# Row norms at stage ends: one matmul against a matrix of ones in place of two one-column matmuls, and the finished reciprocal root kept for all partitions

## The chip, the cores and the metric

One core of a Trainium2 chip runs the whole program. The metric is the device time of one launch in microseconds. The kernel before took 3085.26 us in the median of three runs (3084.18 to 3092.69). The two levels of the TensorE clock are 1.2 and 2.4 GHz; the profile gives them as 0.5 and 1.0 of the granted clock.

## The reference

Two network blocks follow each other on x of [256 tokens, 1024 features]. Each sublayer begins with an RMS norm over the features:

```python
def rmsnorm(x, g):
    xf = x.astype(jnp.float32)
    y = xf * lax.rsqrt(jnp.mean(xf * xf, axis=-1, keepdims=True) + RMS_EPS)
    return y.astype(x.dtype) * g

# first block, for two layers (mixers: hgrn + gmlp, then mla + moba attention)
x = x + mixer(x); x = x + peer_ffn(x, norm_ffn, ...)
# second block, for two layers (m are modulations; the layer-0 mixer reads a context ctx too)
x = x + 0.5 * m[2] * swiglu(modulate(x, norm_g[l, 0], m[0], m[1]), ffn1_wi[l], ffn1_wo[l])
x = x + m[5] * mixer(modulate(x, norm_g[l, 1], m[3], m[4]))      # window + gla, then a pooling mixer
x = x + 0.5 * m[8] * swiglu(modulate(x, norm_g[l, 2], m[6], m[7]), ffn2_wi[l], ffn2_wo[l])
return rmsnorm_2(x, final_g)
```

`modulate` is an RMS norm with a gain and a shift. The layer-0 swiglu ahead of the window mixer runs on the 256 rows of ctx as well.

## The kernel before

Features lie on partitions: x is `K.x`, [128, 8 chunks, 256 tokens] in SBUF, and stays there from start to end. The program is a sequence of stages. Each stage has its own semaphores and one instruction stream per engine, and all engines meet at a barrier between stages. Every big product is three fp32r products of high and low halves: ScalarE makes the high half of a weight tile with a copy (L262), VectorE or GpSimd the low half with a subtraction (L266), and TensorE multiplies (L2758, L2837 and others). Inside a stage TensorE is the engine that is always busy.

A norm needs, for each token, one over the root of the mean square over all 1024 features, and it needs that number on every partition, since tokens lie along the free axis. At nine places the sum of squares is made at the end of the stage that writes x (class `RowNorm`, slot 0 for x and slot 1 for ctx):

- VectorE writes a chunk of x (L3030, L2058, L797 or L3519); ScalarE squares it (L468); GpSimd adds chunks 0+1, 2+3 and 4+5 (L451).
- TensorE sums over the partitions (L461): for each of the three pairs and for chunks 6 and 7, two matmuls, one for each 128 tokens, with the squares as weights and one column of ones as the moving operand. The result is [128 tokens, 2]: a token lies on a partition.
- ScalarE takes the root of these 128x2 numbers (L472), VectorE the reciprocal (L476). Then comes the barrier.

In the next stage class `KnownNorm` spreads the result: TensorE multiplies a broadcast of the reciprocal with the identity (L418), which puts [128 partitions, 256 tokens] into PSUM. VectorE waits for that (L368) and then scales x chunk by chunk (L369): x times the gain times the spread reciprocal. ScalarE adds the shift and rounds to the high half (L357, or L262 where there is no shift), VectorE makes the low half of it (L382), in some stages GpSimd for the odd chunks (L266 and L393).

There are eight boundaries with such a norm: into `l_in`, `ffn1_0`, `wg_in` (two norms), `ffn2_0`, `ffn1_1`, `pool`, `ffn2_1` and `finish`. In the four `ffn` stages (function `swiglu`) ScalarE first makes the high halves of two weight tiles (L262, two of 128x1024) and then the chunks of the norm; GpSimd makes the low halves of these two weight tiles (L266, its only work there); TensorE multiplies the high parts chunk by chunk as the norm delivers them (function `highs`, L2758). Both `tensor` parts issue a few dummy products with the identity (`keep_awake`, L279), one at each stage's end and some at its start. In `l_in` and `wg_in` (function `project`) GpSimd makes the first weight tile's low half, and after it the odd chunks of the norm.

Of the kernel before, what the change touches and what calls it, by code (L numbers as in the profile page):

```python
# [17 lines left out]
P = 128  # L18
# [150 lines left out]
def setup(nc, keep, dram, K):  # L169

    taken = 0

    def sb(name, shape, dt=F32):
        nonlocal taken
        tile, size = padded(nc, keep, name, shape, dt, 64)
        taken += size
        return tile

    K.x = sb("x_stream", [P, DC, T])
    K.xp = sb("x_normed", [P, 2, DC, T], F32R)  # L180
    K.cols = sb("cols", [P, NCOL])
    K.ones = sb("ones", [P, P])
    K.ident = sb("ident", [P, P])
    K.iota = sb("iota", [P, P])
    K.eps = sb("eps", [P, 1])
    K.lb = sb("lower_bound", [P, AH])
    K.nlb = sb("one_less_lower_bound", [P, AH])
    K.mod = [sb(f"mod{n}", [P, MT, 2 - n]) for n in range(2)]
    K.row_root, K.row_inverse = sb("row_root", [P, 2, TT]), sb("row_inverse", [P, 2, TT])
    K.inv_freq = sb("inv_freq", [P, 32])  # L190
    K.cos, K.sin = sb("cos", [P, TT, 32]), sb("sin", [P, TT, 32])
    if (taken + MOVED) % LINE:
        sb("setup_end", [P, (LINE - (taken + MOVED) % LINE) // 4])

    K.raw = tile_in_lines(nc, keep, "raw", [P, RAWS, D])
    K.col = lambda name: K.cols[:, COL_AT[name][0]:COL_AT[name][1]]
    K.row = lambda name: K.rows[:, ROW_AT[name][0]:ROW_AT[name][1]]

    with stage(nc, K.stages, "setup") as st:
        cols_in, x_in, freq_in = st.sem("cols_in"), st.sem("x_in"), st.sem("freq_in")  # L200
        filled, v_step, exped = st.sem("filled"), st.sem("v_step"), st.sem("exped")
        cleared, shifted = st.sem("cleared"), st.sem("shifted")
        e = st.sb("e", [P, 3, AH])
        mx = st.sb("mx", [P, AH])
        mx2 = st.sb("mx2", [P, AH])
        spare = st.ps("spare", [P, P])
        block = st.ctx.enter_context(nc.Block())

        @block.tensor
        def _(pe):  # L210
            pe.wait_ge(filled, 1)
            keep_awake(pe, K, spare[:], 8)

        @block.sync
        def _(sp):
            sp.dma_start(K.cols[:], dram["cols"]).then_inc(cols_in, 16)
            sp.dma_start(K.x[:], dram["x"]).then_inc(x_in, 16)
            at = ROW_AT["inv_freq"]
            sp.dma_start(K.inv_freq[:], dram["rows"][at[0]:at[1]].partition_broadcast(P)).then_inc(freq_in, 16)
            sp.wait_ge(x_in, 16)  # L220
            sp.wait_ge(freq_in, 16)

        @block.gpsimd
        def _(pool):
            pool.memset(K.ones[:], 1.0)
            pool.memset(K.eps[:], EPS)
            pool.memset(K.ident[:], 0.0).then_inc(cleared, 1)
            pool.iota(K.iota[:], pattern=[[1, P]], base=0, channel_multiplier=0,
                      allow_small_or_imprecise_dtypes=True)
            pool.wait_ge(cleared, 1)  # L230
            pool.affine_select(out=K.ident[:], in_=K.ident[:], compare_op=ALU.not_equal, fill=1.0,
                               base=0, pattern=[[-1, P]], channel_multiplier=1).then_inc(filled, 1)

        @block.vector
        def _(dve):

            chain = Chain(dve, v_step)
            dve.wait_ge(cols_in, 16)
            lg = K.col("lb_logits").rearrange("p (r h) -> p r h", r=3)
            chain(dve.tensor_tensor(mx[:], lg[:, 0], lg[:, 1], ALU.max))  # L240
            chain(dve.tensor_tensor(mx2[:], mx[:], lg[:, 2], ALU.max))
            dve.tensor_tensor(e[:], lg, mx2[:].unsqueeze(1).to_broadcast([P, 3, AH]),
                              ALU.subtract).then_inc(shifted, 1)
            dve.wait_ge(exped, 1)
            chain(dve.tensor_tensor(mx[:], e[:, 0], e[:, 1], ALU.add))
            chain(dve.tensor_tensor(mx2[:], mx[:], e[:, 2], ALU.add))
            chain(dve.reciprocal(mx[:], mx2[:]))
            chain(dve.tensor_tensor(K.lb[:], e[:, 0], mx[:], ALU.mult))
            chain(dve.tensor_scalar(K.nlb[:], K.lb[:], -1.0, 1.0, ALU.mult, ALU.add))

        @block.scalar
        def _(act):
            act.wait_ge(shifted, 1)
            act.activation(e[:], e[:], ACT.Exp).then_inc(exped, 1)
# [27 lines left out]
class Norm:  # L282
# [67 lines left out]
    def scalar_to(self, act, end):  # L350
# [10 lines left out]
            ins.then_inc(self.cut, 1)  # L361
        self.scalar_at = max(self.scalar_at, end)

    def vector_scale(self, dve, end):

        for n in range(self.scaled_at, end):
            if n == 0:
                dve.wait_ge(self.spread, 1)  # L368
            dve.scalar_tensor_tensor(out=self.sq[:, n], in0=self.src[:, n], scalar=self.gain[:, n:n + 1],  # L369
                                     in1=self.rstd, op0=ALU.mult, op1=ALU.mult).then_inc(self.scaled, 1)  # L370
        self.scaled_at = max(self.scaled_at, end)
# [33 lines left out]
class KnownNorm(Norm):  # L405
# [2 lines left out]

    def __init__(self, st, K, tag, slot, *args, **kwargs):
        super().__init__(st, K, tag, *args, **kwargs)  # L410
        self.inverse = K.row_inverse[:, slot]

    def tensor_sums(self, pe, awake=3):
        pass

    def tensor_spread(self, pe):
        for t in range(self.tokens // P):
            mm = pe.matmul(self.rstd[:, t * P:(t + 1) * P], self.inverse[:, t:t + 1].to_broadcast([P, P]),  # L418
                           self.K.ident[:], start=True, stop=True, skip_group_check=True)
        mm.then_inc(self.spread, 1)  # L420

    def scalar_squares(self, act):
        pass
# [11 lines left out]
class RowNorm:  # L435
# [4 lines left out]

    def __init__(self, st, K, slot, src, sq, total):
        self.K, self.src, self.sq, self.total = K, src, sq, total
        self.root, self.inverse = K.row_root[:, slot], K.row_inverse[:, slot]
        self.stored, self.squared, self.paired, self.summed, self.rooted = (
            st.sem(f"rows{slot}_{x}") for x in ("stored", "squared", "paired", "summed", "rooted"))

# [6 lines left out]
    def tensor_sums(self, pe, c):  # L453
        if c < self.PAIRED:
            if c % 2:
                return
            pe.wait_ge(self.paired, c // 2 + 1)
        else:
            pe.wait_ge(self.squared, c + 1)
        for t in range(TT):  # L460
            mm = pe.matmul(self.total[:, t:t + 1], self.sq[:, c, t * P:(t + 1) * P], self.K.ones[:, 0:1],  # L461
                           start=c == 0 and t == 0, stop=c == DC - 1, skip_group_check=True)
        if c == DC - 1:
            mm.then_inc(self.summed, 1)

# [3 lines left out]

    def scalar_root(self, act):  # L470
        act.wait_ge(self.summed, 1)
        act.activation(self.root, self.total, ACT.Sqrt, bias=self.K.eps[:], scale=1.0 / D).then_inc(self.rooted, 1)  # L472

    def vector_root(self, dve):
        dve.wait_ge(self.rooted, 1)
        dve.reciprocal(self.inverse, self.root)  # L476


class LateNorm(Norm):
# [140 lines left out]
def project(nc, K, name, blocks, sources=lambda st: (), loads=(), ahead=None, ring=None, beside=None, rows=None, following=(),  # L620
# [11 lines left out]
    with stage(nc, K.stages, name) as st:  # L632
# [9 lines left out]
        src = sources(st)  # L642
        early = [s for s in src if not s.late]
        beside = beside and beside(st, src, evacuated, others)
        rows = rows and rows(st, acc[:, 0, 0:TT])
        following = Following(st, following)
        block = st.ctx.enter_context(nc.Block())

# [95 lines left out]
        def _(act):  # L744
# [32 lines left out]
            for b in range(b, len(blocks)):  # L777
                evacuate(b)
            if rows:
                act.activation(K.row_root[:, 0, 0:1], K.eps[:], ACT.Sqrt)  # L780
                for c in range(DC):
                    rows.scalar_square(act, c)
                rows.scalar_root(act)
# [461 lines left out]
def peer_experts(nc, K, name, layer, dram, raw, mix, beside, following):  # L1245
# [40 lines left out]
    with stage(nc, K.stages, f"{name}_e") as st:  # L1286
# [78 lines left out]
        iota_ps, w_low = out[:, 3, 0, 0:P], out[:, 3, 1]  # L1365
        norm_ps = out[:, 2].rearrange("p a t -> p (a t)")
        rstd, total = norm_ps[:, 0:T], norm_ps[:, T:T + TT]
        rows = RowNorm(st, K, 0, K.x, ring[:, 0:2].rearrange("p r (a t) -> p (r a) t", t=T), out[:, 0, 0, 0:TT])
        key_ps = g_ps[:, :, 0:TT * NK].rearrange("p k (t n) -> p k t n", t=TT)
        block = st.ctx.enter_context(nc.Block())  # L1370

# [1307 lines left out]
def swiglu(nc, K, name, wi, wo, streams, at, following=()):  # L2679
# [7 lines left out]
    with stage(nc, K.stages, name) as st:  # L2687
# [17 lines left out]
        def out_ps(s, c):  # L2705
# [5 lines left out]
                           total=acc[:, 7], all_vector=True)]  # L2711
        norms += [Norm(st, K, "n1", x.x, x.gain, x.shift, pair=x.pair, total=acc[:, 6], all_vector=True)
                  for x in streams[1:]]
        rows = [RowNorm(st, K, s, x.x, norms[s].sq, acc[:, 4 * s, 0:TT]) for s, x in enumerate(streams)]
        block = st.ctx.enter_context(nc.Block())

        @block.sync
# [744 lines left out]
def pool_mix(nc, K, dram, M, following):  # L3462
# [3 lines left out]
    with stage(nc, K.stages, "pool") as st:  # L3466
# [7 lines left out]
        acc = st.ps("acc", [P, DC, T])  # L3474
        h = a[:, :, pad:pad + T]
        norm = KnownNorm(st, K, "n", 0, K.x, M.gain(1), M.shift(1), raw=h)
        rows = RowNorm(st, K, 0, K.x, norm.sq, norm.total)
        following = Following(st, following)
        block = st.ctx.enter_context(nc.Block())

# [64 lines left out]
def second_block(nc, K, dram, mods, out):  # L3545
    for layer, M in enumerate(mods):
# [3 lines left out]
        if layer == 0:  # L3550
            with ExitStack() as keep:
                ctx = tile_in_lines(nc, keep, "ctx_stream", [P, DC, T])
                with ExitStack() as wide:
                    ctx_pair = moving_tile(nc, wide, "ctx_wide", [P, 2, DC, T])
                    swiglu(nc, K, "ffn1_0", *weights, [
# [114 lines left out]
```

## Time and profile before

| | |
|---|---|
| median of three runs | 3085.26 us |
| the profiled execution's own time | 3088.12 us |
| its span | 3086.4 us |
| TensorE busy | 3031.7 us, 98% |
| VectorE busy | 2095.9 us, 68% |
| ScalarE busy | 1582.3 us, 51% |
| GpSimd busy | 605.3 us, 20% |
| mean granted TensorE clock | 0.982 |

The span is that of the profiled execution, first to last instruction; the 1.7 us beside it lie around it. Busy times of TensorE are modelled ends of pipelined matmuls, so 98% busy does not say that it is at its peak in every stage. An fp32 matmul (L461, L418, L279, L3531) appears as two records, an fp32r matmul as one.

### The profile page before, as it was taken

How to read it: one execution, taken by the hardware profiler on the slowest of the kernel's cores; microseconds unless marked ns; L12 is line 12 of the kernel's file. 1: busy time of each engine (PE TensorE's matmuls, PEld its weight loads, DVE VectorE, ACT ScalarE, POOL GpSimd, SP SyncE). 2: the span in 40 equal slices, each digit the busy share in tenths (PEclk: the TensorE clock that was granted, in tenths of full speed). 3: DMA queues.
4: the chain of work that ended last, by engine and by line, in shares of the span. 5: the costliest groups of instructions: out<-in, count | busy, mean ns of one | idle time of the engine just before them, and what ended most of it. 6: DMA issues, size and time to landing. Idle time of an engine off the chain costs nothing. (4 is left out here: it accounts for less than half of the span.)

```text
span 3086.4 us, 66249 instructions
## 1 busy us (share of the span) xinstructions
PE 3031.7 (98%) x25756; PEld 2962.7 (96%) x25756; DVE 2095.9 (68%) x3612; ACT 1582.3 (51%) x2760; POOL 605.3 (20%) x327
## 2 busy tenths in 40 slices
PE   9899999999999999999999999999999899999998
PEld 9799999999999799999999999999998799999898
DVE  4669788789996659888778886333255555555654
ACT  5364577655555654577655554222145354454443
POOL 1126377600001016477500000000020000000100
PEclk9999999999999999999999999999999899999999
DMA  5256655688896256655689994223242246565464
GB/s 189 81 162 186 183 164 163 197 260 288 288 370 204 88 158 194 191 164 162 191 286 317 312 318 148 90 95 93 91 117 76 73 148 194 171 192 176 144 196 144
DMA packets 172777, 560.62 MB, mean 182 GB/s; under 512 B 22480, under 2 KB 31440, under 8 KB 172000
## 3 DMA queue, kind: packets, MB, share of 16 engines
q1 hardware_dynamic: 172640, 558.83, 56.3%
q8 instruction: 82, 1.34, 0.2%
q14 instruction: 55, 0.45, 0.0%
HBM read 557.71 MB, written 1.05 MB: 181 GB/s over the span
## 5 line engine op out<-in xcount | busy, mean ns | idle before, releaser
L262 ACT ACTIVATE peer_e_hi<-raw 128x1024 fp32r<-128x1024 f32 x560 | 590.5, 1055 | 313.6 <-PE peer_e_out L1558 256.3
L266 DVE TENSOR_TENSOR ffn_lo<-raw,ffn_hi 128x1024 fp32r<-128x1024 f32 x256 | 312.9, 1225 | 470.8 <-ACT ffn_hi L262 470.8
L262 ACT ACTIVATE ffn_hi<-raw 128x1024 fp32r<-128x1024 f32 x264 | 279.2, 1061 | 531.5 <-PE ffn_acc L2843 337.4
L266 POOL TENSOR_TENSOR peer_e_lo<-raw,peer_e_hi 128x1024 fp32r<-128x1024 f32 x198 | 478.0, 2416 | 286.2 <-ACT peer_e_hi L262 285.6
L266 DVE TENSOR_TENSOR peer_e_lo<-raw,peer_e_hi 128x1024 fp32r<-128x1024 f32 x362 | 444.3, 1227 | 119.6 <-ACT peer_e_hi L262 115.8
L1554 PE MATMUL peer_e_out<-x_normed,peer_e_hi 128*128 128x256 f32 x2048 | 493.6, 283 | 0.0
L1555 PE MATMUL peer_e_out<-x_normed,peer_e_hi 128*128 128x256 f32 x2048 | 481.7, 278 | 0.0
L1624 PE MATMUL peer_e_out<-peer_h_pair,peer_e_hi 128*128 128x256 f32 x2048 | 477.7, 276 | 0.4 <-DVE peer_e_lo L266 0.4
L1625 PE MATMUL peer_e_out<-peer_h_pair,peer_e_hi 128*128 128x256 f32 x2048 | 477.5, 276 | 0.0
L1555 PEld LDWEIGHTS peer_e_out<-x_normed,peer_e_hi 128*128 128x128 f32 x2048 | 385.8, 188 | 0.0
L1554 PEld LDWEIGHTS peer_e_out<-x_normed,peer_e_hi 128*128 128x128 f32 x2048 | 385.3, 188 | 0.2 <-issue 0.2
L1624 PEld LDWEIGHTS peer_e_out<-peer_h_pair,peer_e_hi 128*128 128x128 f32 x2048 | 384.4, 188 | 0.7 <-issue 0.7
L1625 PEld LDWEIGHTS peer_e_out<-peer_h_pair,peer_e_hi 128*128 128x128 f32 x2048 | 384.5, 188 | 0.0
L2838 PE MATMUL ffn_acc<-x_normed,ffn_hi 128*128 128x256 f32 x1280 | 313.5, 277 | 0.0
L2837 PE MATMUL ffn_acc<-x_normed,ffn_hi 128*128 128x256 f32 x1280 | 313.4, 277 | 0.0
L262 ACT ACTIVATE peer_h_pair<-peer_e_h 128x256 fp32r (+1 forms) x256 | 106.8, 418 | 334.6 <-PE peer_e_out L1628 334.6
L1558 PE MATMUL peer_e_out<-x_normed,peer_e_lo 128*128 128x256 f32 x2048 | 276.6, 277 | 0.5 <-POOL peer_e_lo L266 0.5
L1628 PE MATMUL peer_e_out<-peer_h_pair,peer_e_lo 128*128 128x256 f32 x2048 | 276.0, 276 | 0.0
L1558 PEld LDWEIGHTS peer_e_out<-x_normed,peer_e_lo 128*128 128x128 f32 x2048 | 253.2, 188 | 1.3 <-POOL peer_e_lo L266 0.9
L1628 PEld LDWEIGHTS peer_e_out<-peer_h_pair,peer_e_lo 128*128 128x128 f32 x2048 | 252.1, 188 | 0.0
L2837 PEld LDWEIGHTS ffn_acc<-x_normed,ffn_hi 128*128 128x128 f32 x1280 | 240.8, 188 | 0.0
L2838 PEld LDWEIGHTS ffn_acc<-x_normed,ffn_hi 128*128 128x128 f32 x1280 | 240.6, 188 | 0.0
(640 smaller groups left out, 6136.7 us busy)
## 6 DMA issues: line engine op xcount, KB each, us to landing
raw<-in_l_down SPq DMA_DIRECT2D x256, 512.0 KB, 3.6
raw<-in_l_up SPq DMA_DIRECT2D x256, 512.0 KB, 4.8
raw<-in_ffn_wi SPq DMA_DIRECT2D x176, 512.0 KB, 3.7
peer_e_ring<-in_w_mod SPq DMA_DIRECT2D x144, 512.0 KB, 5.3
raw<-in_ffn_wo SPq DMA_DIRECT2D x88, 512.0 KB, 3.6
raw<-in_l_peer_w_query SPq DMA_DIRECT2D x32, 512.0 KB, 3.5
raw<-in_w_in SPq DMA_DIRECT2D x26, 512.0 KB, 4.2
l_in_raw<-in_l_w_in SPq DMA_DIRECT2D x24, 512.0 KB, 4.4
```

The lines of the kernel that those rows point to most:

```text
L262: return act.activation(hi, v, ACT.Copy)
L266: return eng.tensor_tensor(lo, v, hi.bitcast(F32), ALU.subtract)
L1554: pe.matmul(out, w, K.xp[:, 0, c], start=c == 0, stop=False)
L1555: pe.matmul(out, w, K.xp[:, 1, c], start=False, stop=False)
L1558: mm = pe.matmul(out, lo[:, k % 2, c * P:(c + 1) * P], K.xp[:, 0, c], start=False, stop=c == DC - 1)
L1624: pe.matmul(out[:, c, 0], w, h_hi[:, k % 2], start=first, stop=False, skip_group_check=True)
L1625: pe.matmul(out[:, c, 0], w, h_lo[:, k % 2], start=False, stop=False, skip_group_check=True)
L1628: return pe.matmul(out[:, c, 0], lo[:, k % 2, c * P:(c + 1) * P], h_hi[:, k % 2], start=False, stop=False, skip_group_check=True)
L2837: pe.matmul(at, w, x.pair[:, 0, c], start=c == 0 and s == 0, stop=False, skip_group_check=True)
L2838: pe.matmul(at, w, x.pair[:, 1, c], start=False, stop=False, skip_group_check=True)
```

## The change

The matmuls of `RowNorm.tensor_sums` are turned round: the whole 128x128 matrix of ones is the weight and the squares stream through it, 256 columns, so every partition receives the sum of every token. Root and reciprocal are then taken of 128x256 numbers. The result is kept in SBUF (`K.row_rstd`, 1 KB a partition for x; another for ctx), and `KnownNorm` uses it as it lies: its spread matmuls and VectorE's wait for them are gone, and L369 reads the reciprocal root from SBUF instead of PSUM. Places that only follow (PSUM rooms of 256 columns instead of 2) are left out below.

```diff
-    K.row_root, K.row_inverse = sb("row_root", [P, 2, TT]), sb("row_inverse", [P, 2, TT])
+    K.row_rstd = [sb("row_rstd", [P, T])]
...
+    def wait_rstd(self, dve):
+        dve.wait_ge(self.spread, 1)
+
     def vector_scale(self, dve, end):
         for n in range(self.scaled_at, end):
             if n == 0:
-                dve.wait_ge(self.spread, 1)
+                self.wait_rstd(dve)
             dve.scalar_tensor_tensor(out=self.sq[:, n], in0=self.src[:, n], scalar=self.gain[:, n:n + 1],
                                      in1=self.rstd, op0=ALU.mult, op1=ALU.mult).then_inc(self.scaled, 1)
...
 class KnownNorm(Norm):
-        self.inverse = K.row_inverse[:, slot]
+        self.room, self.rstd = self.rstd, K.row_rstd[slot][:]
     def tensor_spread(self, pe):
-        for t in range(self.tokens // P):
-            mm = pe.matmul(self.rstd[:, t * P:(t + 1) * P], self.inverse[:, t:t + 1].to_broadcast([P, P]),
-                           self.K.ident[:], start=True, stop=True, skip_group_check=True)
-        mm.then_inc(self.spread, 1)
+        pass
+    def wait_rstd(self, dve):
+        pass
...
 class RowNorm:
-        self.root, self.inverse = K.row_root[:, slot], K.row_inverse[:, slot]
+        self.rstd = K.row_rstd[slot][:]
     def tensor_sums(self, pe, c):
-        for t in range(TT):
-            mm = pe.matmul(self.total[:, t:t + 1], self.sq[:, c, t * P:(t + 1) * P], self.K.ones[:, 0:1],
-                           start=c == 0 and t == 0, stop=c == DC - 1, skip_group_check=True)
+        mm = pe.matmul(self.total, self.K.ones[:], self.sq[:, c], start=c == 0, stop=c == DC - 1,
+                       skip_group_check=True)
     def scalar_root(self, act):
-        act.activation(self.root, self.total, ACT.Sqrt, bias=self.K.eps[:], scale=1.0 / D).then_inc(self.rooted, 1)
+        act.activation(self.rstd, self.total, ACT.Sqrt, bias=self.K.eps[:], scale=1.0 / D).then_inc(self.rooted, 1)
     def vector_root(self, dve):
-        dve.reciprocal(self.inverse, self.root)
+        dve.reciprocal(self.rstd, self.rstd)
```

## Rows read from the trace of the kernel before

**Rows 1.** The page, busy time, share and instructions of TensorE and VectorE.
```profile
PE 3031.7 (98%) x25756; PEld 2962.7 (96%) x25756; DVE 2095.9 (68%) x3612; ACT 1582.3 (51%) x2760; POOL 605.3 (20%) x327
```

**Rows 2.** Line view of L476: durations in ns, then what VectorE waited for (us, times).
```profile
L476 DVE RECIPROCAL row_inverse<-row_root x9: 166/166/168, 957.8 to 3076.2; 128x2 f32<-128x2 f32 x9
...
  ACT row_root L472: 21.6, 9
```

**Rows 3.** Timeline of TensorE, ffn2_0 into ffn1_1: start, us, line, [idle before <-releaser].
```profile
2671.48 2.15 PE L461 MATMUL ffn_acc<-ones,ffn_n_sq 128*128 128x1 f32 x12 [0.18 <-POOL ffn_n_sq L451]
...
2674.56 1.20 PE L418 MATMUL ffn_acc<-ident,row_inverse 128*128 128x128 f32 x4 [0.30 <-PEq L146]
...
2676.99 3.30 PE L2758 MATMUL ffn_acc<-x_normed,ffn_hi 128*128 128x256 f32 x16 [0.38 <-ACT x_normed L357]
```

**Rows 4.** Timeline of ScalarE, the same boundary.
```profile
2673.67 0.26 ACT L472 ACTIVATE row_root<-ffn_acc,eps 128x2 f32<-128x2 f32 x1 [2.25 <-PE ffn_acc L461]
2674.54 2.00 ACT L262 ACTIVATE ffn_hi<-raw 128x1024 fp32r<-128x1024 f32 x2 [0.61 <-PEq L146]
2676.45 3.29 ACT L357 ACTIVATE x_normed<-ffn_n_sq,mod 128x256 fp32r<-128x256 f32 x8
```

**Rows 5.** Timelines of VectorE and GpSimd, the same boundary.
```profile
2673.96 0.17 DVE L476 RECIPROCAL row_inverse<-row_root 128x2 f32<-128x2 f32 x1 [3.00 <-ACT row_root L472]
2675.80 3.22 DVE L369 SCALAR_TENSOR_TENSOR ffn_n_sq<-x_stream,mod,ffn_acc 128x256 f32<-128x256 f32 x8 [1.67 <-PE ffn_acc L418]
2678.93 4.52 DVE L382 SCALAR_TENSOR_TENSOR x_normed<-ffn_n_sq,mod,x_normed 128x256 fp32r<-128x256 f32 x8
...
2675.67 4.72 POOL L266 TENSOR_TENSOR ffn_lo<-raw,ffn_hi 128x1024 fp32r<-128x1024 f32 x2 [4.24 <-ACT ffn_hi L262]
```

**Rows 6.** Line views of VectorE's reciprocals L518 and L1968: ns min/median/max, shapes.
```profile
L518 DVE RECIPROCAL hgrn_heads_rstd<-hgrn_heads_root x1: 203/203/203, 128.8 to 128.8; 128x8 f32<-128x8 f32 x1
...
L1968 DVE RECIPROCAL peer_e_dens<-peer_e_dens x2: 253/253/253, 363.5 to 1287.4; 128x16 f32<-128x16 f32 x2
```

**Rows 7.** Timeline of TensorE: last sums at the pool boundary; fp32 matmuls of 256 columns.
```profile
2859.81 1.50 PE L461 MATMUL ffn_acc<-ones,ffn_n_sq 128*128 128x1 f32 x12 [0.18 <-POOL ffn_n_sq L451]
...
2877.69 1.99 PE L3531 MATMUL pool_acc<-pool_pooled,pool_w 128*128 128x256 f32 x8 [1.17 <-DVE pool_pooled L3514]
```

**Rows 8.** Line view of L3531: ns min/median/max of one record.
```profile
L3531 PE MATMUL pool_acc<-pool_pooled,pool_w x32: 379/379/483, 2874.6 to 2884.0; 128*128 128x256 f32 x32
```

**Rows 9.** Line views of L369, L382 and GpSimd's L266, start of ffn2_0.
```profile
L369 DVE SCALAR_TENSOR_TENSOR ffn_n_sq<-x_stream,mod,ffn_acc x8: 472/473/480, 2487.5 to 2490.2; 128x256 f32<-128x256 f32 x8
...
L382 DVE SCALAR_TENSOR_TENSOR x_normed<-ffn_n_sq,mod,x_normed x8: 472/472/1739, 2490.6 to 2494.7; 128x256 fp32r<-128x256 f32 x8
...
L266 POOL TENSOR_TENSOR ffn_lo<-raw,ffn_hi x2: 2374/2383/2392, 2487.4 to 2489.7; 128x1024 fp32r<-128x1024 f32 x2
```

**Rows 10.** Timelines of VectorE and GpSimd at the start of peer1.
```profile
1066.12 2.74 DVE L266 TENSOR_TENSOR x_normed<-peer_mix,x_normed 128x256 fp32r<-128x256 f32 x3
...
1065.00 4.46 POOL L266 TENSOR_TENSOR x_normed<-peer_mix,x_normed 128x256 fp32r<-128x256 f32 x4 [37.70 <-ACT x_normed L262]
```

**Rows 11.** Granted clock by stretch: us, busy (x) of the engines, PEclk, DMA share, GB/s.
```profile
2672.20:2678.80 6.60, 5.92 (x26) 5.36 (x26) 3.17 (x9) 4.52 (x9) 3.13 (x2) 0.50 0.00 1
2273.50:2283.50 10.00, 9.96 (x44) 8.21 (x45) 10.00 (x17) 7.89 (x16) 2.75 (x4) 1.00 0.78 211
...
962.10:965.40 3.30, 3.27 (x15) 3.30 (x16) 2.99 (x7) 1.98 (x4) 2.20 (x3) 0.50 0.56 159
```

**Rows 12.** Timelines: VectorE at the start of l_in, TensorE's last sums before wg_in.
```profile
960.28 1.71 DVE L382 SCALAR_TENSOR_TENSOR x_normed<-l_in_n_sq,x_normed 128x256 fp32r<-128x256 f32 x1
...
2264.72 3.97 PE L461 MATMUL ffn_acc<-ones,ffn_n_sq 128*128 128x1 f32 x24
```

**Rows 13.** Timeline of VectorE: the pool stage's wait, and the start of finish.
```profile
2870.53 2.43 DVE L3509 TENSOR_TENSOR pool_b<-pool_a 128x2176 f32<-128x2176 f32 x1 [1.92 <-DMA pool_inv<-in_pool_inv]
...
3078.04 1.26 DVE L369 SCALAR_TENSOR_TENSOR finish_n_sq<-x_stream,cols,finish_n_total 128x256 f32<-128x256 f32 x3 [1.66 <-PE finish_n_total L418]
```

More of the change, by code:

```diff
@@ L644, in project @@
         beside = beside and beside(st, src, evacuated, others)
-        rows = rows and rows(st, acc[:, 0, 0:TT])
+        rows = rows and rows(st, acc[:, 0, 0:T])
         following = Following(st, following)
@@ L779, in _ @@
             if rows:
-                act.activation(K.row_root[:, 0, 0:1], K.eps[:], ACT.Sqrt)
+                act.activation(K.row_rstd[0][:, 0:1], K.eps[:], ACT.Sqrt)
                 for c in range(DC):
@@ L1367, in peer_experts @@
         rstd, total = norm_ps[:, 0:T], norm_ps[:, T:T + TT]
-        rows = RowNorm(st, K, 0, K.x, ring[:, 0:2].rearrange("p r (a t) -> p (r a) t", t=T), out[:, 0, 0, 0:TT])
+        rows = RowNorm(st, K, 0, K.x, ring[:, 0:2].rearrange("p r (a t) -> p (r a) t", t=T), out[:, 0, 0])
         key_ps = g_ps[:, :, 0:TT * NK].rearrange("p k (t n) -> p k t n", t=TT)
@@ L2713, in swiglu @@
                   for x in streams[1:]]
-        rows = [RowNorm(st, K, s, x.x, norms[s].sq, acc[:, 4 * s, 0:TT]) for s, x in enumerate(streams)]
+        rows = [RowNorm(st, K, s, x.x, norms[s].sq, acc[:, 4 * s, 0:T]) for s, x in enumerate(streams)]
         block = st.ctx.enter_context(nc.Block())
@@ L3476, in pool_mix @@
         norm = KnownNorm(st, K, "n", 0, K.x, M.gain(1), M.shift(1), raw=h)
-        rows = RowNorm(st, K, 0, K.x, norm.sq, norm.total)
+        rows = RowNorm(st, K, 0, K.x, norm.sq, norm.room)
         following = Following(st, following)
@@ L3552, in second_block @@
                 ctx = tile_in_lines(nc, keep, "ctx_stream", [P, DC, T])
+                K.row_rstd.append(tile_in_lines(nc, keep, "ctx_rstd", [P, T]))
                 with ExitStack() as wide:
```

## The prediction

> **What bounds the kernel now.** I read the page's busy times first [rows 1]: TensorE is busy in 98% of the span. The reader should take from it that inside the stages nothing else sets the pace, and that what is not TensorE's dense work lies at stage boundaries. The change touches only these. So I read the line view of the last instruction of a stage, the reciprocal [rows 2]: nine of them, 166 ns each, and VectorE stands idle for 21.6 us in all before them, 2.4 us each. There the program is a single chain: the last sums on TensorE, the root on ScalarE, the reciprocal, the barrier. Then I read one boundary engine by engine, ffn2_0 into ffn1_1, which four of the eight resemble. TensorE [rows 3]: the last 12 sum records start at 2671.48, the spread at 2674.56, the first product of the new stage at 2676.99, released by the first normed chunk from ScalarE (L357). ScalarE [rows 4]: the new stage starts at 2674.54 with two weight cuts that last 2.00 us, and L357 follows at 2676.45 without a gap. VectorE [rows 5] waits 1.67 us for the spread, and its first scaled chunk is ready at 2676.27, just before ScalarE is free. So the spread is hidden behind ScalarE's two cuts, and from the barrier on ScalarE is the bound: 8 chunks in 3.29 us, which is also the pace of TensorE's 16 products (3.30 us).
>
> **What lengthens the end of a stage.** In order along the chain:
>
> - Reciprocal. 128x2 takes 166 ns, 128x8 203, 128x16 253 [rows 2, 6]. That is 6.2 ns for each element of the free axis (87 ns over 14 elements). For 256 elements: 253 + 240 x 6.2 = 1.75 us, +1.59 us. The bounds: an L369 of the same shape takes 0.47 us [rows 9] if the slope were that of an ordinary operation, and 1.95 is a tenth above the line, which is drawn out sixteenfold here. I take 1.75, because all three sizes lie on the line. The row's slope is several times that of an ordinary operation. The Trainium skill (VectorE: DVE Perf Modes, First, the fixed hardware budget) says that the reciprocal is an iterated divide with a repeat count of 8; at the 0.96 GHz that the page gives, an estimate by it is 8.3 ns an element and 2.3 us, which would put 0.5 us more on each boundary than the rows do.
> - Root. 128x2 takes 0.26 us [rows 4]; L357, of 128x256, follows its like every 0.41 (3.29 over 8). I take 0.43, +0.17; bounds +0.1 and +0.25.
> - Sums. The last three summands follow GpSimd's last addition without a gap: 12 records, 1.50 us at full clock before pool [rows 7] and 2.15 where the clock fell to half in their middle [rows 3]. New: 6 records of 256 columns. L3531 is such an fp32 matmul: 8 records in 1.99 us, of which the last one's latency is 0.38 [rows 7, 8], so they stand 0.23 us apart, and 6 take 5 x 0.23 + 0.38 = 1.5 us. So no gain at full clock, and up to 0.65 where it used to fall, since the array is now fed 256 columns at a time. Over seven boundaries I take 0.25 on average; bounds 0 and 0.65.
>
> That makes +1.5 us for seven boundaries. The one into wg_in differs: 24 records take 3.97 us [rows 12], half of them at half clock; streamed they end about 1.2 us earlier, but the two 1.75 us reciprocals, x and ctx, now queue on VectorE. Net +0.9. Together 7 x 1.5 + 0.9 = 11.4 us; every engine stands at the barrier meanwhile, so all of it counts. In pool what comes next is a DMA that is issued after the barrier and ends last, 1.92 us after VectorE is ready [rows 13], so the shift passes through there too.
>
> **What the removed spread gives back.** In finish there is no ScalarE or GpSimd work: VectorE waits 1.66 us for the spread [rows 13], of which the barrier takes 0.4 (the reciprocal ends at 2674.13, ScalarE starts at 2674.54 [rows 4, 5]); it starts some 1.25 us earlier. That is -1.25. In the four ffn stages it gives nothing (ScalarE's cuts, above). In l_in and wg_in TensorE waits for L382 of the first chunk, which starts at 960.28 and takes 1.71 us instead of 0.47: it stands behind GpSimd's weight tile [rows 12], and would from an earlier start too. 0 in both, and in pool, where the DMA ends last [rows 13].
>
> **What the SBUF operand costs.** This is the largest term. L369 reads the spread from PSUM, and its eight took 472 to 480 ns although GpSimd was subtracting weight tiles all that time; L382, with both tensors in SBUF, took 472 but once 1739 ns: it started at 2490.6 and ended at 2492.3, 0.2 us behind the end of GpSimd's second instruction (2489.7 and 2.39 more) [rows 9]. So a VectorE instruction with two SBUF tensors stands while GpSimd's runs. Where both have a queue they take turns: in peer1 three such subtractions take 2.74 us, 0.9 each instead of 0.4, beside GpSimd's four in 4.46 [rows 10]. L369 now reads two SBUF tensors. Put into ffn1_1, counted from ScalarE's first cut at r = 2674.54: VectorE no longer waits and scales chunks 0, 1, 2 by r+1.3. GpSimd wants its first tile at r+1.13 and gets it when chunk 2 has passed; chunk 3 stands until r+3.6 and is done at 3.9; GpSimd's second tile goes next, to r+6.2; chunk 4 is done at 6.5, chunk 7 at 7.7. L357 of chunk 7 ends at about r+8.3 instead of r+5.2 [rows 4], and TensorE's first pass, which takes the chunks in order, ends 3.2 us later. After it TensorE has no slack: the second pass needs L382, which now meets no GpSimd and ends at r+10.9, before TensorE asks for it. +3.2 us in each of four stages, 12.8. Bounds: 0 if the turn goes to VectorE for its whole queue and GpSimd loses nothing that counts, and 3.6 if one chunk less passes at first. In wg_in L369 meets GpSimd's odd chunks, a quarter of a weight tile each, 0.6 us by [rows 9]; +0.7, and 0.1 in l_in. Term: 13.6.
> The row shows one instruction that stands to the end of GpSimd's. The Trainium skill (SBUF — State Buffer, Who interferes with whom) has the rule for it: a VectorE instruction with two SBUF inputs contends with a GpSimd one that reads SBUF, and the holder blocks the other for its whole length. By that rule, too, this change is to be slower in the four stages; the rows give the size.
>
> **The clock.** It is at half from 2672.2 to 2678.8 [rows 11]: it fell in the one-column sums and rose only when TensorE had been at the products for some 2 us. Before, this cost nothing in an ffn stage, where ScalarE sets the pace of these products anyway. Now TensorE has some 9 us with little to do from the end of the sums to chunk 4, the clock will be low when the dense work starts, and part of it will run at half: I take +1.0 us for each ffn stage (bounds 0 and 2.5). In wg_in the products ran at full clock from the first (1.00 from 2273.5 on [rows 11]), which spread and dummies had brought about: +1.5. In l_in dense work already ran at half for 3.3 us [rows 11] and may gain or lose 1.6: 0. Term: 5.5.
>
> **Sum.** 11.4 - 1.25 + 13.6 + 5.5 = 29.3 us. The profiled execution had 3088.12 us (span 3086.4 and 1.7 around it) and would have 3117; it lies 2.9 above the median of the three runs, so for the median I say 3085.3 + 29 = 3114 us.
>
> **Rivals.**
> - *No contention in L369.* If the kept row (the same for every chunk) or its read order spares it, 12.8 + 0.8 go, and most of the clock's term: 11.4 - 1.25 + 2 = +12, 3097 us. For it: nothing in the trace shows L369 with this operand. Against it: L382 has the same form and stood.
> - *It is not slower.* The mechanism is the reciprocal and the clock together: if the reciprocal of 128x256 takes the 0.47 us of an ordinary operation, a boundary's end grows by 0.3 + 0.17 - 0.25 = 0.2, and since TensorE now streams 256 columns until the root, the clock may hold over the shorter pause: l_in gains 1.6, finish 1.25, and L369 escapes GpSimd because it starts 1.25 us earlier. 1.5 - 2.85 = -1.4, 3084 us. It decides from a reciprocal under 0.5 us. For it: the pause is one spread shorter. Against it: three sizes on a steep line, and three chunks are all that pass before GpSimd starts.
> - *A longer stall.* The reciprocal at its upper bound (8 x 0.2), one chunk less before GpSimd (4 x 0.4) and 2.5 us of clock in four stages (4 x 1.5): +9 on the forecast, 3123 us. Mechanism as forecast, sizes at their upper bounds.
>
> **Chances.** Forecast 0.60, no contention 0.17, not slower 0.10, longer stall 0.13. Since 0.3% (9.3 us, about what a measurement of this kernel tells from none) lies below the second case, slower has 0.84, within 0.3% 0.13, faster 0.03. The range goes from 3096 to 3125: the lower end takes in most of the no-contention case, the upper the long stall.
>
> **What would show it.** In the profile after: L476 with 128x256 near 1.75 us (over 1.4 or my first term is wrong); L472 near 0.43; L461 as two records a summand, 0.23 us apart, the clock still 1.0 at their end; no L418. In each ffn stage L369 no longer at 0.47 throughout, but with two of about 2.4 us, and L357 idle before chunks 3 and 4 with VectorE as releaser. TensorE's 16 first products spread over about 6.5 us instead of 3.3. If L369 stays at 0.47, the rival is true; if GpSimd's L266 grows instead, the turns go the other way round and the stall is smaller.

## The result and the profile after

The kernel after takes 3104.39 us in the median of eight runs (3097.64 to 3116.39), the kernel before 3083.54 us in eight runs beside it (3073.83 to 3092.69). The ratio is 1.0074, with a 95% interval of 1.0050 to 1.0099: slower by 21 us, between 15 and 31. The profiled execution of after took 3100.99 us (span 3099.3).

The line views of after come first: durations in ns (least, median, most), first and last start, shapes. They answer to [rows 2] and [rows 9].

```profile
L478 DVE RECIPROCAL row_rstd<-row_rstd x8: 1752/1753/1754, 953.1 to 3088.8; 128x256 f32<-128x256 f32 x8
...
L474 ACT ACTIVATE row_rstd<-peer_e_out,eps x2: 473/473/473, 952.5 to 1878.0; 128x256 f32<-128x256 f32 x2
...
L372 DVE SCALAR_TENSOR_TENSOR ffn_n_sq<-x_stream,mod,row_rstd x32: 472/480/2593, 1880.9 to 2903.8; 128x256 f32<-128x256 f32 x32
L372 DVE SCALAR_TENSOR_TENSOR wg_in_n_sq<-x_stream,mod,row_rstd x8: 473/484/979, 2260.9 to 2270.7; 128x256 f32<-128x256 f32 x8
```

The reciprocal is at 1.753 us, where the line through three sizes had it. The root takes 0.47 us. The scaling (now L372) has a median of 480 ns and a longest of 2593.

The boundary ffn2_0 into ffn1_1 again, in the timelines of after (start, us, line, idle time before it and its releaser). They answer to [rows 3], [rows 4] and [rows 5]. TensorE:

```profile
2670.17 1.56 PE L463 MATMUL ffn_acc<-ffn_n_sq,ones 128*128 128x256 f32 x6
2671.57 0.38 PE L279 MATMUL ffn_acc<-ident 128*128 128x128 f32 x2
2674.33 0.68 PE L279 MATMUL ffn_acc<-ident 128*128 128x128 f32 x4 [2.38 <-PEq L146]
2676.77 1.65 PE L2760 MATMUL ffn_acc<-x_normed,ffn_hi 128*128 128x256 f32 x6 [1.75 <-ACT x_normed L357]
2678.71 0.80 PE L2760 MATMUL ffn_acc<-x_normed,ffn_hi 128*128 128x256 f32 x2 [0.30 <-ACT x_normed L357]
2681.20 2.07 PE L2760 MATMUL ffn_acc<-x_normed,ffn_hi 128*128 128x256 f32 x8 [1.69 <-ACT x_normed L357]
2683.07 1.91 PE L2760 MATMUL ffn_acc<-x_normed,ffn_lo 128*128 128x256 f32 x8
2684.78 4.76 PE L2760 MATMUL ffn_acc<-x_normed,ffn_hi 128*128 128x256 f32 x32
2689.37 1.07 PE L2760 MATMUL ffn_acc<-x_normed,ffn_lo 128*128 128x256 f32 x8
```

ScalarE, VectorE and GpSimd:

```profile
2671.77 0.47 ACT L474 ACTIVATE row_rstd<-ffn_acc,eps 128x256 f32<-128x256 f32 x1 [1.67 <-PE ffn_acc L463]
2674.31 2.00 ACT L262 ACTIVATE ffn_hi<-raw 128x1024 fp32r<-128x1024 f32 x2 [2.07 <-PEq L146]
2676.22 1.29 ACT L357 ACTIVATE x_normed<-ffn_n_sq,mod 128x256 fp32r<-128x256 f32 x3
2678.15 0.51 ACT L357 ACTIVATE x_normed<-ffn_n_sq,mod 128x256 fp32r<-128x256 f32 x1 [0.64 <-DVE ffn_n_sq L372]
2680.64 1.71 ACT L357 ACTIVATE x_normed<-ffn_n_sq,mod 128x256 fp32r<-128x256 f32 x4 [1.98 <-DVE ffn_n_sq L372]
...
2674.33 7.46 DVE L372 SCALAR_TENSOR_TENSOR ffn_n_sq<-x_stream,mod,row_rstd 128x256 f32<-128x256 f32 x8 [0.30 <-PEq L146]
...
2675.45 4.87 POOL L266 TENSOR_TENSOR ffn_lo<-raw,ffn_hi 128x1024 fp32r<-128x1024 f32 x2 [5.33 <-ACT ffn_hi L262]
```

The reader is to see four things. The sums end at full clock and cost 1.56 us, as at the pool boundary before. ScalarE waits for the barrier (2.07 us instead of 0.61) while VectorE divides. VectorE's eight scalings take 7.46 us instead of 3.22, and ScalarE waits ahead of chunks 3 and 4, released by VectorE. And TensorE, with holes of 1.75, 0.30 and 1.69 us ahead of and inside its first products, starts the dense work at half clock: eight products in 1.91 us that take 1.07 a little later. The windows view has the granted clock (after the busy times):

```profile
2676.60:2686.20 9.60, 7.45 (x31) 6.86 (x32) 9.60 (x15) 6.51 (x12) 3.72 (x2) 0.50 0.32 111
```

**A trap in the comparison of two profiles.** The two profiled executions differ by 12.9 us, while their boundaries alone, laid side by side, differ by 30.6. Inside ffn1_0, in a loop where no instruction was changed, the execution of after is 13 us faster (353.5 and 340.4 us), and some 5 us more lie ahead of the first boundary. TensorE's records in 280 us of that stage, before and then after (us, busy, records, clock):

```profile
1960.00:2240.00 280.00, 280.00 (x2380) 1.00 0.30 94
```

```profile
1960.00:2240.00 280.00, 280.00 (x2473) 1.00 0.31 96
```

Both are busy throughout at full clock, but 93 records more get through. Experiments 1 and 5 are about this. For all that follows I therefore use **turns** and not spans: the time from GpSimd's last addition of a stage to the first product of the next stage's steady loop (in `l_in` to its first product; for finish to the end). They leave the dense bodies out, with two exceptions: the turns of pool (26 us) and wg_in (217 us) run to GpSimd's next last addition, and wg_in's holds the whole window mixer with its dense work. That one is therefore rough: the three profiles of before already lie 1.0 us apart in it.

### The profile page after: what moved, and what is told of

Same layout as the page of the kernel before. It is cut to its first block and busy times, and to the rows that moved or that the text cites. A ratio compares the mean times of both kernels' runs of the same rounds, so it can differ in the third digit from the quotient of the medians.

```text
span 3099.3 us, 65996 instructions
## 1 busy us (share of the span) xinstructions
PE 3011.6 (97%) x25630; PEld 2935.1 (95%) x25630; DVE 2126.0 (69%) x3612; ACT 1584.7 (51%) x2760; POOL 606.1 (20%) x327
## 5 line engine op out<-in xcount | busy, mean ns | idle before, releaser
L266 DVE TENSOR_TENSOR ffn_lo<-raw,ffn_hi 128x1024 fp32r<-128x1024 f32 x256 | 312.9, 1225 | 458.3 <-ACT ffn_hi L262 458.3
L266 POOL TENSOR_TENSOR peer_e_lo<-raw,peer_e_hi 128x1024 fp32r<-128x1024 f32 x198 | 478.0, 2416 | 283.8 <-ACT peer_e_hi L262 283.2
L266 DVE TENSOR_TENSOR peer_e_lo<-raw,peer_e_hi 128x1024 fp32r<-128x1024 f32 x362 | 444.1, 1227 | 117.9 <-ACT peer_e_hi L262 113.9
```

The costliest lines, as they stand in the source:

```text
L266: return eng.tensor_tensor(lo, v, hi.bitcast(F32), ALU.subtract)
```

## Experiments

All times are medians, with the ratio to the kernel before run beside them. The turns are worked out from the timelines, from one profile of each kernel. "One-stream turn" is the mean of ffn2_0, ffn1_1 and ffn2_1; "all turns" is the sum over the eight boundaries. "Before x3" is the mean of three profiles with the instructions of before (the shown one, experiments 1 and 5), whose sums are 348.4, 349.3 and 350.5 us.

| kernel | one-stream turn | all turns | against before | measured ratio (95%) |
|---|---|---|---|---|
| before x3 | 17.8 us | 349.4 us | | |
| after | 23.6 | 379.0 | +29.6 | 1.0074 (1.0050 to 1.0099) |
| 1 addresses alone | 17.9 | 349.3 | -0.1 | 0.9983 (0.9959 to 1.0007) |
| 2 factors read from PSUM | 19.6 | 361.1 | +11.7 | 1.0040 (1.0016 to 1.0064) |
| 3 reciprocal alone | 19.2 | 360.6 | +11.2 | 1.0026 (1.0001 to 1.0051) |
| 4 one root | 21.6 | 363.5 | +14.0 | 1.0029 (1.0009 to 1.0050) |
| 6 turn filled | 23.5 | 378.9 | +29.5 | 1.0064 (1.0036 to 1.0092) |
| 7 GpSimd later | 26.4 | 385.2 | +35.8 | 1.0106 (1.0045 to 1.0167) |
| 8 narrow root | 17.9 | 346.9 | -2.5 | 0.9997 (0.9964 to 1.0030) |
| 9 holes filled | 21.7 | 370.3 | +20.9 | 1.0085 (1.0056 to 1.0114) |
| 10 one root and PSUM | 17.4 | 346.3 | -3.1 | 1.0010 (0.9989 to 1.0031) |
| 11 narrow root, filled | 17.4 | 346.0 | -3.4 | 1.0000 (0.9977 to 1.0024) |

**1. Addresses alone.**

```diff
+    sb("room", [P, T - 32])
...
+                tile_in_lines(nc, keep, "ctx_room", [P, T])
```

> Kernel before, no instruction changed: only the two pieces of on-chip memory that the change takes are taken too (960 bytes more a partition in the setup, 1 KB before the wide ctx tile of ffn1_0), unused. Theory A (addresses): the body of ffn1_0, from its first L2837 product to its end, falls from 353 us to about 340 us as in the kernel after, and the time is about 3083.5 - 13 = 3070 us. Theory B (chance between executions, or an effect of the change's own instructions): the body stays at 353 us and the time within 0.3% of 3083.5 us.

Measured: 3076.89 us, ratio 0.9983, the turns those of before, and ffn1_0's body at 340.5 us. By itself that spoke for theory A. Experiment 3, with the addresses of before, had 340.5 as well, so the fast rate does not need the new addresses; experiment 5 settles it.

**2. The factors read from PSUM.** Kernel after, with one identity product back.

```diff
     def tensor_spread(self, pe):
-        pass
-
-    def wait_rstd(self, dve):
-        pass
+        pe.matmul(self.rstd, self.K.ident[:], self.kept, start=True, stop=True,
+                  skip_group_check=True).then_inc(self.spread, 1)
```

> Kernel after, but the next stage first copies the kept factors from SBUF to PSUM with one identity product on TensorE (128x256, about 0.4 us and two hops), and VectorE's first pass (L372) reads them there, as in the kernel before. Theory A (the SBUF operand makes VectorE's first pass meet GpSimd): the eight L372 of the stages with one row stream take 3.2 to 3.8 us instead of 7.45; four such stages give back 4 x 4.6 us, the window stage 2, and eight copies cost about 0.7 each: 3104.4 - 20.4 + 5.6 = 3089.6 us. Theory B (the operand's place is no cause; L372 is slow for another reason): eight L372 stay at 7.4 us, and the time rises by 8 x 0.7 to about 3110 us.

Measured: 3093.33 us (3089.6 expected). The timeline of VectorE at the same boundary:

```profile
2662.46 1.75 DVE L476 RECIPROCAL row_rstd<-row_rstd 128x256 f32<-128x256 f32 x1 [2.63 <-ACT row_rstd L472]
2665.65 3.22 DVE L372 SCALAR_TENSOR_TENSOR ffn_n_sq<-x_stream,mod,ffn_acc 128x256 f32<-128x256 f32 x8 [1.44 <-PE ffn_acc L420]
```

The eight scalings are at 3.22 us again, with the wide reciprocal still ahead of them. Theory A stands: with GpSimd at work as before, the operand's place decides between 7.46 and 3.22. The turn falls by 4.0 us.

**3. The reciprocal alone.** Kernel before, with a 128x256 reciprocal ahead of the narrow one.

```diff
         dve.wait_ge(self.rooted, 1)
+        dve.reciprocal(self.sq[:, 1], self.sq[:, 1])
         dve.reciprocal(self.inverse, self.root)
```

> Kernel before with one instruction more in each of the eight row norms: a reciprocal of 128x256 on VectorE over squares that nobody reads again, right ahead of the narrow one. All else stays, the factors are spread into PSUM as before. Theory A (terms add): each boundary is 1.75 us longer, L369 stays at 3.2 us for eight, the time is 3083.5 + 14 = 3097.5 us. Theory A2 (the longer idle of TensorE also moves the granted clock): the stretch at half clock in the four stages of one or two row streams grows from 6.8 to 10.2 us although L369 is fast, +1.4 each: 3103 us. Theory B (the reciprocal is hidden behind the stage's turn): under 3090 us.

Measured: 3086.17 us, ratio 1.0026. By the time alone theory B (under 3090) was met: the medians differ by 3 us, and the interval reaches from 0.3 to 15.7 us. The turns speak against it: they are 11.2 us longer in sum, and 13.0 without wg_in, whose 215.3 us lie under all three profiles of before although two reciprocals were added there. So the reciprocal is not hidden, and theory A's 14 was a little high. The stretch at half clock after the turn was 6.8, 6.8 and 10.2 us in the one-stream stages and 10.2 in ffn1_0, so A2 is half right: it grew in two of four.

**4. One root.** Kernel after; reciprocal and root become one ScalarE activation.

```diff
-        act.activation(self.rstd, self.total, ACT.Sqrt, bias=self.K.eps[:], scale=1.0 / D).then_inc(self.rooted, 1)
+        act.activation(self.rstd, self.total, ACT.Abs_reciprocal_sqrt, bias=self.K.eps[:], scale=1.0 / D)
...
-        dve.wait_ge(self.rooted, 1)
-        dve.reciprocal(self.rstd, self.rstd)
+        pass
...
-                act.activation(K.row_rstd[0][:, 0:1], K.eps[:], ACT.Sqrt)
+                act.activation(K.row_rstd[0][:, 0:1], K.eps[:], ACT.Abs_reciprocal_sqrt)
```

The last two lines load the function's table ahead of time; three other places follow in the same way.

> Kernel after, with the root and the reciprocal of the row norms replaced by one ScalarE activation (the reciprocal square root), so VectorE's reciprocal of 128x256 and the hop to it are gone from all eight. Theory A (they end last): 8 x 1.95 = 15.6 us less, 3088.8 us, and near 3083 if the half-clock stretch of the ffn stages falls back from 10.2 to 6.8 us as well. Theory B (half clock comes from VectorE's slow first pass and stays): 3088.8. Theory C (a table load of about a microsecond enters each boundary): 3097 us or more.

Measured: 3092.71 us; the turns fall by 15.6 us, the 8 x 1.95 expected. The activation takes what the root took, and no table load enters between the sums and the next stage. The program has 35 table loads (1.28 us each) instead of 32, since other norms still use Sqrt; the three further ones lie in `l_in`, in ffn1_0 behind its first products, and in wg_out ahead of its squares. The stretch at half clock fell back to 6.8 us in ffn2_0 (turn 20.7 us) and stayed at 10.2 in ffn1_1 and ffn2_1 (22.3 and 21.9). ScalarE and VectorE at the same boundary:

```profile
2661.51 0.47 ACT L474 ACTIVATE row_rstd<-ffn_acc,eps 128x256 f32<-128x256 f32 x1 [1.67 <-PE ffn_acc L463]
2662.26 2.00 ACT L262 ACTIVATE ffn_hi<-raw 128x1024 fp32r<-128x1024 f32 x2 [0.27 <-PEq L146]
...
2662.28 7.46 DVE L372 SCALAR_TENSOR_TENSOR ffn_n_sq<-x_stream,mod,row_rstd 128x256 f32<-128x256 f32 x8 [2.89 <-PEq L146]
```

ScalarE starts the stage 0.27 us after the root instead of 2.07; L372 keeps its 7.46. So the reciprocal and the slow scaling are separate costs.

**5. The kernel before, profiled again.** No edit.

> The kernel before, unchanged, profiled a second time. Theory A (each execution of one program falls into one of two rates in the dense body of ffn1_0, a median of 0.118 or 0.113 us from product to product, about 353.5 or 340.4 us for the body, by chance): the body can be either; if it is 340.4, the profile shown of before and this one differ by 13 us with not one instruction changed. Theory B (the slow rate belongs to the kernel before): 353.5 again. Either way the boundaries of the three stages with one row stream take 17.4 to 18.2 us from GpSimd's last addition to the first product of the body.

Measured: 3076.93 us in its one run, and ffn1_0's body 340.5 us instead of 353.5. The same windows view, this execution first and the kernel of experiment 8 behind it:

```profile
1960.00:2240.00 280.00, 280.00 (x2473) 1.00 0.31 98
```

```profile
1960.00:2240.00 280.00, 280.00 (x2380) 1.00 0.29 92
```

So one program has either count: the kernel before had the low one in its first profile and the high one here. The stages with one row stream have two rates as well. In this single execution ffn2_0 (first line) runs at one and ffn1_1 at the other, 532 against 512 records in 60 us, 170.5 against 177.0 us a body:

```profile
2490.00:2550.00 60.00, 60.00 (x532) 1.00 0.60 194
2680.00:2740.00 60.00, 60.00 (x512) 1.00 0.58 186
```

Of 13 profiles four had the slow rate in ffn1_0 (13 us each), and of 39 one-stream bodies seven (6.5 us each), among the relatives of before and of after alike. Theory A stands; what picks the rate stays open.

**6. The turn filled.** Kernel after, with more dummy products.

```diff
-                keep_awake(pe, K, acc[:, 0, 512:512 + P], 1)
+                keep_awake(pe, K, acc[:, 0, 512:512 + P], 8)
...
-            keep_awake(pe, K, acc[:, 0, 0:P], 2)
+            keep_awake(pe, K, acc[:, 0, 0:P], 9)
...
-            keep_awake(pe, K, acc[:, 1, 0:P], 1)
+            keep_awake(pe, K, acc[:, 1, 0:P], 8)
```

> Kernel after, with identity products on TensorE filling the turn of the stages: 8 instead of 1 after the row sums, 9 instead of 2 ahead of the first real product of the ffn stages, all into banks that hold nothing. Theory A (part of the loss is the granted clock, half of full for 10.2 us instead of 6.8 in each ffn stage because TensorE waits longer): the half-clock stretches shrink or move, and each of the three one-stream stages goes from 23.6 us to about 22.2; over all 3104 - 6 = 3098 us. Theory B (the clock costs nothing since the start waits for VectorE and ScalarE anyway): 23.6 stays, time within 3 us of 3104.

Measured: 3104.18 us, turn 23.5: theory B's number. But the half-clock stretch had only shrunk and moved: it was 3.4, 6.8 and 3.4 us long in the one-stream stages instead of 10.2, in ffn1_1 it began 9.5 us after GpSimd's last addition instead of 6.5, inside the holes of the first products, and in all three it lay over the dense start all the same (eight products 1.91 us). Its window in ffn1_1:

```profile
2686.30:2693.00 6.70, 5.17 (x24) 5.18 (x25) 6.70 (x14) 5.09 (x8) 0.65 (x1) 0.50 0.35 128
```

So the run did not show that the clock costs nothing; experiment 9 asks again.

**7. GpSimd later.** Kernel after; GpSimd starts its two weight tiles when VectorE has scaled all chunks.

```diff
+            pool.wait_ge(norms[0].scaled, DC)
             for j in range(2):
                 pool.wait_ge(hi_1, j + 1)
```

> Kernel after, where GpSimd starts the two low parts of the first weights (L266) in the ffn stages only when VectorE has finished its eight L372 of the first row stream. Theory A (GpSimd's L266 is what stretches L372 to 2.59 us): eight L372 take 3.2 to 3.9 us with no instruction over 0.6, while they still read the factors from SBUF; the low parts come 4 us later and TensorE may wait for them, so the one-stream stages end between 19.6 and 22.5 us instead of 23.6. Theory B (the SBUF operand alone, or ScalarE's traffic, is the cause): L372 stays at 7.4 us, and the stage is 4 us longer, 27.5 us.

Measured: 3114.16 us in four runs. The same boundary, line views of L372 and of GpSimd's L266, and TensorE's timeline:

```profile
L372 DVE SCALAR_TENSOR_TENSOR ffn_n_sq<-x_stream,mod,row_rstd x8: 479/480/486, 2672.5 to 2675.3; 128x256 f32<-128x256 f32 x8
...
L266 POOL TENSOR_TENSOR ffn_lo<-raw,ffn_hi x2: 2365/4961/7557, 2675.9 to 2683.4; 128x1024 fp32r<-128x1024 f32 x2
```

```profile
2674.98 3.48 PE L2760 MATMUL ffn_acc<-x_normed,ffn_hi 128*128 128x256 f32 x16 [1.75 <-ACT x_normed L357]
2683.49 2.07 PE L2760 MATMUL ffn_acc<-x_normed,ffn_lo 128*128 128x256 f32 x8 [5.03 <-POOL ffn_lo L266]
```

With GpSimd out of the way L372 takes 0.48 us each although it reads the factors from SBUF. The operand alone costs nothing; it needs GpSimd beside it. The stage is longer all the same, 26.4 us, beyond theory A's 22.5, since now GpSimd loses the turns: its first tile lasts 7.56 us, beside an unbroken row of ten VectorE instructions (eight L385 in 3.25 us and two L266 in 2.35, all with two tensors in SBUF), and TensorE waits 5.03 us for it. Here the two did not take turns as in [rows 10]; what decides that stays open.

**8. The narrow root.** Kernel before, with experiment 4's activation on 128x2 (its table is loaded ahead of time as there).

```diff
-        act.activation(self.root, self.total, ACT.Sqrt, bias=self.K.eps[:], scale=1.0 / D).then_inc(self.rooted, 1)
+        act.activation(self.inverse, self.total, ACT.Abs_reciprocal_sqrt, bias=self.K.eps[:], scale=1.0 / D)
```

> Kernel before, with the narrow root and reciprocal of the row norms (128x2) replaced by one ScalarE activation (reciprocal square root); sums, spread and the PSUM operand stay as they are. Theory A (the chain root, reciprocal, turn ends last): the reciprocal of 0.17 us and the hops around it go, 8 x 0.4 = 3 us less than before, 3080 us; the one-stream stages go from 17.6 to about 17.2 us. Theory B (something else ends last): no difference that can be measured.

Measured: 3080.81 us, ratio 0.9997. The turns are 2.5 us shorter in sum, of which the one-stream stages have nothing (17.9): no gain that can be told. Theory A's 17.2 did not come.

**9. The holes filled too.** Experiment 6, and in the first products:

```diff
                         mul(0, j, hi[:, j], s, 0, c, first=c == 0 and s == 0)
+                    if s == 0 and c in (2, 3):
+                        keep_awake(pe, K, acc[:, 3, 0:P], 2 if c == 2 else 7)
```

> Kernel after with identity products on TensorE filling the turn of the stages as in the run before (8 after the row sums, 9 ahead of the first product) and, new, the two holes inside the first products of the ffn stages (2 after chunk 2, 7 after chunk 3, where VectorE's 2.59 us instructions leave TensorE idle for 0.64 and 1.99 us). Theory A (about 1.8 us of each one-stream stage's loss is the granted clock: eight products 1.91 instead of 1.07 us, thirty-two 4.7 instead of 3.8): the half-clock stretch is gone from there or falls ahead of the products, and the stages take 21.8 instead of 23.6 us; the whole 3104 - 7 = 3097 us. Theory B (half clock stays, or costs nothing): 23.4 us as in the run with the turn filled alone.

Measured: turn 21.72, 21.72 and 21.71 us, theory A's 21.8. The whole is 3102.09 us; its interval (+17 to +35 us) cannot tell the 7 us, and the profiled execution had the slow ffn1_0. The timeline of TensorE in ffn1_1, and its windows view:

```profile
2693.98 1.71 PE L2760 MATMUL ffn_acc<-x_normed,ffn_hi 128*128 128x256 f32 x8 [0.43 <-ACT x_normed L357]
2695.52 1.08 PE L2760 MATMUL ffn_acc<-x_normed,ffn_lo 128*128 128x256 f32 x8
2696.43 3.79 PE L2760 MATMUL ffn_acc<-x_normed,ffn_hi 128*128 128x256 f32 x32
```

```profile
2687.00:2705.00 18.00, 17.08 (x136) 16.03 (x137) 15.75 (x22) 11.89 (x19) 4.90 (x2) 1.00 0.39 130
```

The clock is 1.00 throughout, and the dense start takes 1.08 and 3.79 us instead of 1.91 and 4.76. So half clock costs the kernel after 1.9 us in such a stage. The stall of L372 is still there; what is gone is TensorE's idle time, so it is this idle time, in the turn and in the holes that the stall makes, that goes with the half clock.

**10. One root and PSUM.** Experiments 2 and 4 together.

> Kernel after with both of its costs taken back: the root and reciprocal in one ScalarE activation, and the kept factors copied into PSUM by one identity product ahead of VectorE's first pass. The streaming sums and the kept tile stay. Theory A (reciprocal and SBUF operand are the whole loss, and they add): the one-stream stages go from 23.6 by 2.0 and 4.0 to 17.6 us, as in the kernel before, and the whole is within 0.3% of before, 3084 us. Theory B (a third cost hides in the change): the stages stay over 18.5 us and the time over 3093.

Measured: 3080.82 us, ratio 1.0010, turn 17.4 us. VectorE in ffn1_1, and the windows view of that turn:

```profile
2665.80 3.22 DVE L372 SCALAR_TENSOR_TENSOR ffn_n_sq<-x_stream,mod,ffn_acc 128x256 f32<-128x256 f32 x8 [3.60 <-PE ffn_acc L420]
```

```profile
2662.60:2681.00 18.40, 16.42 (x119) 15.10 (x119) 13.77 (x23) 12.20 (x21) 4.79 (x3) 1.00 0.41 122
```

Nothing of the loss is left, with the streaming sums and the kept tile still in place: theory B falls, and no third cost is needed beside the two and the clock that hangs on them. It is a balance and not a return to before, though: the clock is 1.00 through all three one-stream turns, where the kernel before has a half-clock stretch of 6.8 us in each (one in [rows 11]). With the narrow sums and the same activation (experiment 8) that stretch is there in all three, so the streaming sums, or the one product of 256 columns in place of the spread, give something back. Which of the two, and how much, no run separates.

**11. The narrow root, and a filled turn.** Experiment 8 with 3 and 5 dummy products in place of 1 and 2, the candidate for a version under both.

> Kernel before with the narrow reciprocal square root on ScalarE, and some identity products more at the turn (3 instead of 1 after the row sums, 5 instead of 2 ahead of the first product in the ffn stages), the candidate for a version under both. Theory A (0.4 to 0.9 us in each ffn stage is half clock in its first products): the one-stream stages go from 17.9 to 17.2 us and the whole is about 3 us under before, less than this measurement tells from no change. Theory B (the products delay the turn or the clock is not moved): 17.9 us or more.

Measured: 3078.65 us, ratio 1.0000, turn 17.4. The turns are 3.4 us shorter in sum, which a timing cannot confirm. No version was measurably faster than the kernel before.

## Why the prediction was right

It said slower by 29 us and 3114 us; the turns are longer by 29.6 us, the medians differ by 21 (15 to 31), and the time is 3104.4. The mechanism came as forecast; that the sum of the turns agrees to 0.3 us is in part luck, since the stall was forecast 0.35 us a stage too high and the ends and the clock 0.2 and 0.3 too low. By its steps:

- **Ends of the stages, forecast 1.5 us a boundary.** Right. The reciprocal is 1.753 us (forecast 1.75), the root 0.47 (0.43), the sums take 1.56 at full clock (1.5). ScalarE's first cut in the one-stream stages comes 4.19 us after GpSimd's last addition instead of 2.5: +1.7. Experiment 4 takes it out.
- **The removed spread, forecast -1.25 us in finish alone.** Right: finish has the longer end (+1.5) and is 0.5 us longer in all. The scaling no longer waits for L418 there ([rows 13] against 0.30 us after).
- **The SBUF operand, forecast +3.2 us in each ffn stage.** Right in its mechanism, down to the order: three chunks pass, chunks 3 and 4 stand. From ScalarE's first cut to the second pass a one-stream stage is +2.85 us (8.76 instead of 5.91). Experiment 2 (other operand, GpSimd unchanged) and experiment 7 (GpSimd away, same operand) both give 0.48 us an instruction: it takes the two together. The Trainium skill (SBUF — State Buffer, Who interferes with whom) calls the port pair that the two engines share an exclusive lock, and a VectorE instruction with two SBUF inputs needs it when GpSimd reads SBUF; that the holder keeps it for the whole instruction it says of VectorE's two-port modes. The trace agrees, for this form too: the two standing L372 last 2.59 and 2.57 us, and each ends 0.3 us behind the end of an L266 (2.38 and 2.52 us). The 7.56 us of an L266 in experiment 7 are the same from the other side, but there it lost to ten instructions in a row.
- **The clock, forecast +1.0 us in each ffn stage and +1.5 in wg_in.** Mis-sized a little. After the second pass begins a one-stream stage is 1.3 us longer (10.67 instead of 9.40); against an undisturbed clock (experiment 9, 9.07) it is 1.6, and 1.9 with the first pass, of which the kernel before already paid a part. The 1.5 us for wg_in has no run of its own: its turn is 2.4 us longer in all, where 3.1 had been summed up, and that turn is rough.
- **By boundary**, forecast and measured turn: l_in 1.6 and 1.9, the four ffn stages 22.8 and 22.6 (ffn1_0 5.2, the others 17.4), wg_in 3.1 and 2.4, pool 1.5 and 2.1, finish 0.25 and 0.5.
- **The absolute time, 10 us too high.** Of these, 1.7 us lie in the base (3085.26 from three runs, 3083.54 from eight) and 8 in the difference (29 forecast, 21 measured). The interval of 15 to 31 holds the 29.6 us of the turns, so chance may be all of it: one execution can run 13 us slower in ffn1_0 alone, as the profiled one of before did. But experiment 6, whose turns are 29.5 us longer, has an interval of 11 to 28 us. Whether the times fall a little short of the turns, and why, stays open; the profiles show no stretch in which the kernel after saves as much.
- **Rivals.** "No contention" would have left L372 at 0.48 us: it stood at 2.59. "Not slower" needed a reciprocal under 0.5 us: it took 1.753. The longer stall's upper bounds (a reciprocal of 1.95 us, two chunks passing, 2.5 us of clock) were not reached: 1.753, three, and 1.3.

## What to carry to other kernels

A value kept for all partitions is not free because a transfer of it is saved. Making it wide costs a slow operation its full length (here 6.2 ns an element for the reciprocal), and reading it from SBUF in place of PSUM put a GpSimd instruction of 2.4 us in the way here. Before an operand moves from PSUM to SBUF, look up what GpSimd does in the same microseconds and how long one of its instructions is. And compare two profiles by stretches whose instructions differ, never by their spans alone.

## What the runs showed of the hardware

- A dense body runs at one of two rates, at full clock and with the same instructions: 2473 or 2380 records in 280 us (ffn1_0), 532 or 512 in 60 us (one row stream). One execution can have both, in different stages. An estimate from 13 us in ffn1_0 and 6.5 in each of three one-stream bodies is 32 us between an execution with all of them fast and one with all slow, of the 3059 to 3106 us over which the kernel before spreads in all its runs; only the profiled executions show their rate.
- VectorE's reciprocals of 128x8, 128x16 and 128x256 lie on one line: 203, 253, 1753 ns. A second one of 128x256 right behind the first takes 1.70 us (wg_in's boundary), and a 128x2 one behind it 0.11 instead of 0.17 (experiment 3).
- ScalarE's reciprocal square root of 128x256 takes 0.47 us, as the root does (experiment 4).
- Dummy products that filled the turn did not keep the clock up behind holes of 0.64 and 1.99 us in the first products: it stood at 0.50 over the dense start (experiment 6). With dummy products in the holes as well it was 1.00 throughout (experiment 9).
